# Recurrent chunks of 128, modulation sums by transposes a slot later, output weights ahead of x, and a new order of the first FFN unit's and the last tiles' work

## What is computed

```python
mod = jax.nn.silu(c) @ w_ada[l] + b_ada[l]
sh1, sc1, gt1, sh2, sc2, gt2 = [m[:, None, :] for m in jnp.split(mod, N_MOD, axis=-1)]
h = rms_norm(x, g_norm_mix[l]) * (1.0 + sc1) + sh1
proj = h @ w_in[l]                      # hq, hf, hi, hg | aq, ak, av | ga, gb
y_a = hgrn2_mix(hq, hf, hi, hg, lower_bounds[l], g_hg_norm[l])   # gated linear recurrence
y_b = dilated_mixture(aq, ak, av)                                # three groups of four heads
merged = jax.nn.sigmoid(ga) * (y_a @ w_branch_a[l]) + jax.nn.sigmoid(gb) * (y_b @ w_branch_b[l])
x = x + (1.0 + gt1) * (merged @ w_out[l])
h2 = rms_norm(x, g_norm_ffn[l]) * (1.0 + sc2) + sh2
u_gate, u_val = jnp.split(h2 @ w_up[l], 2, axis=-1)
u_gate = causal_dwconv(u_gate, conv_w[l], conv_b[l])
x = x + (1.0 + gt2) * ((jax.nn.gelu(u_gate) * u_val) @ w_down[l])
return rms_norm(x, g_final)
```

## Time and profile before

| | |
|---|---|
| median of 3 runs | 968.55 us (968.55 to 968.78) |
| the profiled execution | 967.42 us, its span 965.7 us |
| TensorE busy | 932.2 us, 97% |
| VectorE, ScalarE, GpSimd busy | 433.2, 360.5, 441.6 us |
| granted TensorE clock, mean | 0.997 of full |
| moved by the transfers | 114.50 MB |

### The profile page before, as it was taken

The page is one execution under the profiler, slowest core; times in us unless marked ns, Lnnn a source line. Parts: engine busy times, 40 slices in busy tenths (PEclk is TensorE's granted clock), DMA queues, the critical chain, the costliest instruction groups (busy, mean ns, idle before and its releaser), DMA issues.

```text
span 965.7 us, 12235 instructions
## 1 busy us (share of the span) xinstructions
PE 932.2 (97%) x4743; PEld 791.7 (82%) x4743; DVE 433.2 (45%) x686; ACT 360.5 (37%) x473; POOL 441.6 (46%) x366
## 2 busy tenths in 40 slices
PE   2999999999999999999999999999999999999996
PEld 2889898988888888878888788888888888888885
DVE  4755466673436978867622625322322222200005
ACT  5423424142334132435322326545544454412113
POOL 1588424334332444245554354744455445544554
PEclk9999999999999999999999999999999999999998
DMA  9833221212143658442524322233222232232212
GB/s 316 274 111 98 78 88 44 88 45 88 44 131 122 215 186 262 155 151 88 203 103 156 127 88 88 88 94 123 87 87 87 98 119 87 87 109 109 88 44 88
DMA packets 93625, 114.50 MB, mean 119 GB/s; under 512 B 2142, under 2 KB 84234, under 8 KB 93582
## 3 DMA queue, kind: packets, MB, share of 16 engines
q1 hardware_dynamic: 93582, 113.89, 35.7%
HBM read 111.76 MB, written 2.12 MB: 118 GB/s over the span
## 4 chain that ended last, share of the span: by engine, by line
PE 42%; issue 31%; POOL 22%; DVE 3%; ACT 1%; DMA 1%; POOLq 0%; SPq 0%; DVEq 0%
PE bank L1018 41%; POOL w_lo L643 19%; DVE bank L1471 1%; POOL xg L696 1%; DMA x_in<-in_x_dram 1%; POOL masks L581 1%; POOL masks L617 1%; ACT h_tmp L748 0%; PE bank L1021 0%; POOL rstd L593 0%; DVE bank L1804 0%; ACT h_hi L751 0%; POOL masks L615 0%; DVE part L1473 0%; DVE xn_ffn L1814 0%
## 5 line engine op out<-in xcount | busy, mean ns | idle before, releaser
L643 POOL TENSOR_TENSOR w_lo<-w_raw,w_hi 128x512 fp32r<-128x512 f32 x292 | 388.0, 1360 | 469.9 <-ACT w_hi L721 464.9
L1018 PE MATMUL bank<-h_hi,w_hi 128*128 128x512 f32 (+1 forms) x848 | 328.1, 390 | 1.7 <-DVE h_lo L1497 1.2
L1018 PE MATMUL bank<-h_lo,w_hi 128*128 128x512 f32 (+1 forms) x848 | 324.7, 386 | 0.0
L1018 PE MATMUL bank<-h_hi,w_lo 128*128 128x512 f32 (+1 forms) x848 | 253.8, 386 | 0.0
L721 ACT ACTIVATE w_hi<-w_raw 128x2048 fp32r<-128x2048 f32 x72 | 137.5, 1910 | 235.2 <-PE bank L1018 235.2
L1018 PEld LDWEIGHTS bank<-h_hi,w_hi 128*128 128x128 f32 x848 | 159.4, 189 | 33.7 <-DVE h_lo L1497 1.4
L1018 PEld LDWEIGHTS bank<-h_hi,w_lo 128*128 128x128 f32 x848 | 159.5, 188 | 32.2
L1018 PEld LDWEIGHTS bank<-h_lo,w_hi 128*128 128x128 f32 x848 | 159.6, 188 | 31.6
L1018 PE MATMUL bank<-w_hi,act_hi 128*128 128x512 f32 x176 | 68.5, 389 | 0.0
L1018 PE MATMUL bank<-w_lo,act_hi 128*128 128x512 f32 x176 | 68.5, 389 | 0.0
L1018 PE MATMUL bank<-w_hi,act_lo 128*128 128x512 f32 x176 | 68.5, 389 | 0.0
(11 more groups left out here) (251 smaller groups left out, 1211.4 us busy)
## 6 DMA issues: line engine op xcount, KB each, us to landing
w_raw<-in_w_in_dram SPq DMA_DIRECT2D x32, 1024.0 KB, 5.2
w_raw<-in_w_up_dram SPq DMA_DIRECT2D x22, 1024.0 KB, 5.1
ada<-in_w_ada_dram SPq DMA_DIRECT2D x16, 1024.0 KB, 5.3
w_raw<-in_w_down_dram SPq DMA_DIRECT2D x11, 1024.0 KB, 4.8
ada<-in_w_ada_dram SPq DMA_DIRECT2D x16, 512.0 KB, 8.7
w_raw<-in_w_out_dram SPq DMA_DIRECT2D x4, 1024.0 KB, 6.9
x_in<-in_x_dram SPq DMA_DIRECT2D x4, 512.0 KB, 5.0
w_raw<-in_w_in_dram SPq DMA_DIRECT2D x8, 256.0 KB, 7.5
```

The costliest lines, as they stand in the source:

```text
L643: ins = pool.tensor_tensor(wlo[slot][:, cols], raw[slot][:, cols], whi[slot][:, cols].bitcast(F32), ALU.subtract)
L1018: return pe.matmul(o, lhsT, rhs, start=start, stop=stop, **kw)
```

## The change

- `CHUNK` becomes 128, so four chunks, each a token tile of its own: `LEVELS` is 7 (a seventh mask, slot 12), the decay and key work moves to slot 13, the updates (three chunks over 128 rows) to slot 14 alone, the output products have 16 products with scores and 12 with states. `q_odd`, its memsets, its copy and its semaphore go.
- Modulation: TensorE transposes the two blocks of sums (two transposes of 128 columns) in the slot after their sums, slots 18 to 28, and VectorE in the slot after that sums over the free axis, waits for its own write and adds the bias. The scales and gate values are made in slot 29. SyncE waits for the last of these transposes ahead of the second row of group weights, whose buffer shares space with the sums.
- SyncE loads unit 38 (output weights) ahead of x and the final gain. In units 36 and 37 VectorE makes the low part of tile f-1 after the sum of tile f, the last one ahead of slot 37's end.
- `last_tiles`, ScalarE's and GpSimd's lists there are reordered; the gating and the adding of one residual are apart, with two feature tiles between; the last token tile is normalised whole on VectorE instead of half on ScalarE; `turned(1)` comes after feature tile 6 instead of 5.
- The end: tile 1 is done in halves too. GpSimd weights only its first half; the second, and the first half of tile 2 and second of tile 3, VectorE does alone. ScalarE squares tiles 0 and 1 ahead of the first scaling, and squares the last half after the scaling of tile 2.

```diff
-CHUNK = 64
+CHUNK = 128
-LEVELS = 6
+LEVELS = 7
-SLOT_KDT, SLOT_UPD, SLOT_O, SLOT_SS = 12, 13, 15, 16
+SLOT_KDT, SLOT_UPD, SLOT_O, SLOT_SS = 13, 14, 15, 16
+OUT_HALVES = ((1, 0), (2, 1), (1, 1), (2, 0), (3, 0), (3, 1))
...
             for u in range(U_UP):
+                if u >= 3:
+                    load_unit(u, unit_source(u), u % 2)
                 if u == U_B + 2:
...
-                if u >= 3:
-                    load_unit(u, unit_source(u), u % 2)
...
                     group_rows(0)
+                    ready(sp, ("mod2", max(MOD_UNITS)))
                     group_rows(1)
...
-            for t in range(TT - 1):
-                root2(t)
+            root2(0)
+            root2(1)
             low_h2(0, 1)
             low_h2(0, 3)
-            root2(TT - 1)
-            for k in range(5, KT, 2):
-                low_h2(0, k)
+            root2(2)
+            low_h2(0, 5)
+            root2(3)
+            low_h2(0, 7)
...
+                        row_square(c, 0)
+                        row_square(c, 1)
+                        xn_again(0, slice(0, D))
+                        high_pair(0, 0)
+                        high_pair(0, 1)
+                        row_square(c, 2)
+                        high_pair(0, 2)
+                        row_square(c, 3)
+                        high_pair(0, 3)
...
-            high_pair(0, 2)
-            xn_again(TT - 1, slice(512, D))
-            high_pair(0, 3)
...
+            for t in range(2):
+                for half in range(2):
+                    square(t, half)
+            act.wait_ge(rstd_done, 2 + TT)
+            scaled_out(0, slice(0, D), y_done)
+            for half in range(2):
+                square(2, half)
+            act.wait_ge(rstd_done, 3 + TT)
+            scaled_out(1, slice(0, 512), y_last[1, 0])
+            square(TT - 1, 0)
+            act.wait_ge(rstd_done, 4 + TT)
+            scaled_out(2, slice(512, D), y_last[2, 1])
+            square(TT - 1, 1)
+            act.wait_ge(rstd_done, 5 + TT)
+            scaled_out(TT - 1, slice(0, 512), y_last[3, 0])
...
                 for t in range(2):
-                    ins = mm(b[:, col + t:col + t + 1], sums[:, t * P:(t + 1) * P], ones[:, 0:1])
+                    cols = slice((col + t) * P, (col + t + 1) * P)
+                    ins = transpose(b[:, cols], sums[:, t * P:(t + 1) * P])
...
-                            ins = mm(b[:, h * P:(h + 1) * P], kd[rows, t, h * P:(h + 1) * P], hv[rows, t, h * P:(h + 1) * P])
+                            ins = mm(b[:, h * P:(h + 1) * P], kd[:, c, h * P:(h + 1) * P], hv[:, c, h * P:(h + 1) * P])
...
-                if u in MOD_UNITS:
+                if u - 1 in MOD_UNITS:
...
-                    if half == 0 and k == 5:
+                    if half == 0 and k == 6:
                         turned(1)
...
+                if u - 2 in MOD_UNITS:
+                    units = MOD_UNITS[u - 2]
+                    b = ready(dve, ("mod2", u - 2))
+                    n = 2 * len(units)
+                    cols = slice(2 * units[0], 2 * units[0] + n)
+                    turned_sums = b[:, 0:n * P].rearrange("p (c q) -> p c q", q=P)
+                    release(dve.tensor_reduce(mod[:, cols], turned_sums, AX_X, ALU.add), ("mod2", u - 2))
+                    evacuated(dve, ("mod2", u - 2))
+                    tt(mod[:, cols], mod[:, cols], vec[:, cols], ALU.add).then_inc(mod2_done, 1)
...
-                        dve.wait_ge(mhi_done, f + 1)
-                        tt(m_lo[:, f, :], sgb[:, f, :], m_hi[:, f, :].bitcast(F32), ALU.subtract).then_inc(mlo_done, 1)
+                        if f:
+                            merged_low(f - 1)
+                    if u == U_OUT - 1:
+                        merged_low(KT - 1)
...
                 xn_again(1, slice(0, D))
-                residual(1, 2)
+                gated(1, 2)
                 make_h2(0, 0)
+                make_h2(0, 2)
+                added(1, 2)
                 low_h2(0, 0)
-                mean_square(2)
-                make_h2(0, 2)
+                make_h2(0, 4)
                 low_h2(0, 2)
                 residual(1, TT - 1)
-                xn_again(2, slice(0, D))
-                make_h2(0, 4)
-                mean_square(TT - 1)
+                mean_square(2)
                 low_h2(0, 4)
                 make_h2(0, 6)
+                xn_again(2, slice(0, D))
+                mean_square(TT - 1)
                 low_h2(0, 6)
-                xn_again(TT - 1, slice(0, 512))
+                xn_again(TT - 1, slice(0, D))
...
             dve.wait_ge(x2_done, 2 * TT)
...
+            first_mean(TT - 1)
+            weighted_out(1, 1)
+            full_mean(TT - 1)
+            weighted_out(2, 0)
+            weighted_out(TT - 1, 1)
```

More of the change, by code:

```diff
@@ L161, in small_products @@
     if u == SLOT_UPD:
-        names += [("upd", c) for c in range(4)]
-    if u == SLOT_UPD + 1:
-        names += [("upd", c) for c in range(4, NCHUNK - 1)]
+        names += [("upd", c) for c in range(NCHUNK - 1)]
     if u == SLOT_O:
@@ L392, in layer_kernel @@
         mean_last = sem("mean_last")
-        y_last = [sem(f"y_tile{t}_half{half}") for t in (TT - 2, TT - 1) for half in range(2)]
+        y_last = {(t, half): sem(f"y_tile{t}_half{half}") for t, half in OUT_HALVES}
         x2_done, y_done, out_done = sem("x2_done"), sem("y_done"), sem("out_done")
@@ L558, in _ @@
             load_unit(N_UNITS - 1, down_rows(FT // 2 - 1), 0)
[L561 to L564, removed]
+            sp.wait_ge(y_done, 1)
+            sp.dma_start(out_tok[:, 0, :], x1[:, 0, :]).then_inc(out_done, 16)
+            for t, half in OUT_HALVES:
                 cols = slice(512 * half, 512 * half + 512)
-                sp.wait_ge(y_last[2 * (t - TT + 2) + half], 1)
+                sp.wait_ge(y_last[t, half], 1)
                 sp.dma_start(out_tok[:, t, cols], x1[:, t, cols]).then_inc(out_done, 16)
-            sp.wait_ge(out_done, 16 * (TT + 2))
+            sp.wait_ge(out_done, 16 * (1 + len(OUT_HALVES)))
         @block.gpsimd
@@ L925, in evacuate, with row_square @@
                     c = (u - U_OUT) // 2
[L926 to L934, removed]
+                    if c == 0:
+                        for t in range(TT):
+                            row_square(c, t)
+                    else:
+                        row_square(c, 0)
[7 more added lines that the diff above has]
+                        high_pair(0, 3)
+            def row_square(c, t):
+                cols = slice(512 * c, 512 * c + 512)
+                evacuated(act, ("out", c, t))
+                act.activation(xn_ffn[:, t, cols], x1[:, t, cols], ACT.Square,
+                               accum_out=ssp[:, 4 * t + c:4 * t + c + 1]).then_inc(ssp_done, 1)
             def xn_again(t, cols):
@@ L1572, in small_results @@
                 if u == SLOT_UPD + 1:
-                    ready(dve, ("kdT", TT - 1))
-                    z_even, z_odd = (a[:, :, :].rearrange("p h (t two c) -> p (h t) two c", two=2, c=CHUNK)
-                                     for a in (zz[0], q_odd))
-                    dve.memset(z_odd[:, :, 0, :], 0.0)
-                    link(dve.tensor_copy(z_odd[:, :, 1, :], z_even[:, :, 1, :]))
-                    dve.memset(z_even[:, :, 1, :], 0.0).then_inc(odd_done, 1)
-                    states(range(4))
-                if u == SLOT_UPD + 2:
-                    states(range(4, NCHUNK - 1))
+                    states()
                 if u == SLOT_O + 1:
```

99 lines of the change are left out of this document (42 added, 57 removed).

## The result

The changed kernel takes 954.77 us (median of four runs, 954.0 to 955.56) beside 968.66 us of the kernel before on the same chip (968.55 to 969.11): a ratio of 0.9858, 95% interval 0.9846 to 0.9869, 13.9 us less. The forecast was 956.9 us, range 954.8 to 960.5. The profiled execution took 955.26 us, its span is 953.5 us: 12.2 us less than the span before.

The account below looks back on a forecast made before the run. TensorE, busy 97% of the span, was taken as the bound. Terms 2.6 + 3.8 + 2.3 + 1.6 + 1.3 = 11.6 us bring the profiled 967.42 to 955.8; the median, 1.1 above, 956.9 us; range 954.8 to 960.5.

Parts of the forecast that it names:

- Recurrence, work: TensorE's recurrence products: seventh level +3.6 us, updates over 128 rows -2.1, fewer output products -3.6; in all -2.1 us.
- Recurrence, waits: TensorE's 1.6 us wait in slot 12 goes; 1.1 us behind VectorE's decay chain in slot 13 comes: -0.5 us.
- Modulation: Transposes in place of one-column products on TensorE, -2.8 us, and a wait removed by the later slot, 1.0: -3.8 us.
- The rival by columns: Modulation on TensorE: streamed columns set the cost, so the 2.8 us gain becomes +0.2; 959.9 us, chance 0.03.
- Output weights: TensorE's wait at the first output product goes through VectorE's later low parts and the earlier loads: -2.3 us, bounds 0 and -2.4.
- First FFN unit: TensorE's waits in the first FFN unit fall from 2.8 to 1.2 us by reordered work: -1.6 us, bounds 0 and -2.8.
- Tail: After TensorE's last product, halved tile work lets the last store leave earlier: -1.3 us, bounds 0 and -1.7.
- the first (waits in place of the removed): Slot 13's chain ends 1.5 us later, or the FFN unit keeps its 1.6 us: 958.4 to 960.0 us, chance 0.16.
- The second: At the first output product, ScalarE's copy stays behind the fourth tile and the 2.3 us stay: 959.2 us, chance 0.06.
- The fourth: The clock falls between slots 18 to 28 as transposes replace products; the kernel gets slower, 979 us for two slots' worth; chance 0.02.
- the fifth rival: Whole kernel: all the terms' bounds turn out good together, 954.5 us; chance 0.03.
- the signs of being wrong: Slot 13's chain ending after 230 us, output weights copied after 538, or granted clock not 1.00 between 30 and 950 us.

Follow-up runs that it names:

- wide ones: The kernel before with the modulation's one-column products made 128 columns wide, the same 64 instructions: 967.61 us, ratio 0.9997.
- the merge alone: The kernel before with only VectorE's low part of each merged tile moved after the next tile's sum, loads in old order: 965.80 us, ratio 0.9971.
- the two groups of executions above: Kernel before with only the output weights loaded ahead of x (968.84 us): four executions took 967.52 to 967.79 us, six 968.67 to 969.66 us.

## Why the prediction was right

The forecast 956.9 was 2.1 us above the 954.77 measured, which is just the lower end of its range, 954.8. The mechanism of each part was right but for one step on the loads and one from profile to median; most sizes were somewhat off. The sum was 11.6 us; the stretches that the change touches give 12.8 (12.2 and the 0.64 of the start). The difference of 1.2 is itself what is left of misses that cancel: the recurrence and the modulation gave 2.1 us more than forecast, the output weights, the FFN unit and the tail 0.9 less. Term by term:

- **Recurrence, work: right.** Forecast -2.1, measured -2.28: the level +3.56 (+3.6), the updates 4.94 to 2.67 (4.8 to 2.7), the outputs 9.83 to 6.25 (to 6.3). An update over 128 rows costs 0.111 us an instruction, as the bound from the level products had it and not the 0.086 of 64 rows. The Trainium skill (TensorE: Matmul & The Clock Gate, "LDWEIGHTS") would have rows not matter; the two spacings differ by 0.025 us here, with the same columns, though the operands' places differ too, so that the rows alone are not shown to be the cause.
- **Recurrence, waits: right in kind, too small.** Forecast -0.5 by 1.6 to 1.1. The wait of slot 12 went, and one for the chain came in slot 13, as forecast; it is 0.56 us instead of 1.1. This trace starts 0.64 us later than the one before. With that taken off, TensorE came at 227.5 (forecast 227.6), but the chain began at 215.3 and not 216.0 and ended at 227.7 and not 228.4, so the wait of 0.8 was 0.3; the 0.3 that I had added for the second key bank was 0.26. Some 0.4 us more of the -3.79 are in rows that differ by less than 0.15 us each; I have no cause for them.
- **Modulation: right, mis-sized by 0.9.** The wait term was 1.0 and is 0.97. The work term was 2.8 and is 3.8: I took 0.109 us for a transpose, from a run of sixteen; a pair between large products adds 0.14 us and four 0.36. The rival by columns had no part (wide ones: no change), and half as many instructions at the old price would have been 0.18 and 0.40 us, so their number accounts for most of it; whether a transpose is also cheaper than a product by itself was not tested. I had priced the rival by a table of the Trainium skill (TensorE: Matmul & The Clock Gate, "Back-to-back issue gap") in which the spacing grows with the columns. The same section gives that table for a product by itself, and says that in a stream of weight loads and products both set the spacing, about 81 ns for 128 columns. The trace is nearer to that: 1 and 128 columns both take 0.37 us for four, 0.09 each.
- **Output weights: right in size and engine, wrong in one step.** -2.3 forecast, -2.29 measured, and ScalarE's fourth tile as the key. "Now the loads matter too" was wrong: without the new order of loads nothing changes, in the change and with the merge alone. I had read the weights as landing at 536.2 from the end of a stretch with transfers in it, which isn't the end of the one transfer: the trace of the kernel before has them issued at 523.21 and landed 11.4 us later, at 534.6, ahead of ScalarE's copy at 538.54 there and at 536.23 with the merge alone. What I did not forecast is the second output unit, late by 0.38 us: I followed the wait to the first unit and not to the next one behind it.
- **First FFN unit: right.** -1.6 forecast, -1.38 measured, bounds held. The step that was off is "hardly at all": the transposes of the second half wait 0.57 us, as VectorE's last row tile took 1.22 us beside GpSimd's low part, where the same operation took 0.75 us elsewhere.
- **Tail: right, 0.3 short.** -1.3 forecast, -1.01 measured. GpSimd's last root took 0.99 us, beside VectorE's write, instead of 0.54 elsewhere in the tail; I had priced it by the latter.
- **The step from profile to median: wrong, and the reason for about half of the 2.1 us.** I added the 1.1 us between the profiled execution and the median of the kernel before to the changed kernel as well. But these are the executions of the kernel before in which the clock halves behind the 2.1 us wait; with the wait they go too. 12.8 + 1.1 is 13.9, the difference of the medians. This reading rests on four of six traces, on the two groups of executions above, and on one median made for it; that the wait brings the falls is well supported, how often it does is known only roughly. Why it does so in some executions and not in others no run shows.

Of the rivals, the first (waits in place of the removed) happened in small: 0.56, 0.38 and 0.57 us. The second, that the merge doesn't do what it says, and the third are out. The fourth had the sign wrong. The clock does move in this kernel, but it fell behind a wait amid large products, not by transposes, so that the change removes the falls. The time lies where the forecast meets the fifth rival (954.5), but not for that rival's reason: the tail, the FFN unit and the wait in slot 13 did not reach their good bounds. Of the signs of being wrong one came true to the letter: the granted clock is 0.50 from 948 to 950 us. TensorE's last product ended at 945.55, so it cost nothing, as 960 to 963 us in the earlier trace rows; the sign should have ended with the last product.

## What to carry to other kernels

When a wait of TensorE goes, follow the same chain to the next unit, and ask what the clock did behind the wait: a wait that takes 2.1 us in the trace can cost 3.7 in another execution. For float32 products of up to 128 columns count instructions, not columns. Price an operation of GpSimd or VectorE by a row that has the other engine's work beside it, if it will have that in its new place.

## What the runs showed of the hardware that I had not expected

- The granted clock fell to half for some 3.4 us in four of six traces after TensorE had stood 2.13 us amid large products, at 1.6 us a time, and did not in the other two; after stands of 1.49 us (with `turned(1)` at tile 5), 1.23 and 0.82 us no such fall was seen.
- A float32 product of one column costs what one of 128 columns does: 0.37 us for four instructions, 0.81 for eight.
- Transposes of float32 cost 0.07 to 0.09 us each when two or four of them stand between large products, 0.104 to 0.109 in runs of fourteen and sixteen.
- VectorE's scaling of 128x1024 took 1.22 us beside GpSimd and 0.75 alone; GpSimd's four pieces of low part took 5.04 us with VectorE idle, 5.94 and 6.40 with its work beside them, and its root of 128 values 0.54 or, beside a write of VectorE, 0.99 us.
